# Moving the decode and attention steps that a decoder kernel weaves between its projection matmuls

## The reference

```python
x = _half_ffn(x, ffn1_norm, ffn1_in, ffn1_out)
h = _rmsnorm(x, mix_norm)
qa, ka, va, qr, kr, vr, gr, ga, gb = jnp.split(h @ w_in, SPLIT_POINTS, axis=-1)
...                       # QK norm, partial rotary
oa, kv_new = attend_a(qa, ka, va)      # dilated window attention, 3 groups x 8 heads x 64
orr, s_new = _retention(qr, kr, vr, s0, chunk)
ob = _rms_plain(orr).reshape(B, T, R_V_W) * jax.nn.silu(gr)
m = sigmoid(ga) * (oa.reshape(B, T, A_HEADS * A_HEAD_DIM) @ w_pa) + sigmoid(gb) * (ob @ w_pb)
x = x + (m @ w_o)
x = _half_ffn(x, ffn2_norm, ffn2_in, ffn2_out)
```

## Time and profile before

| | us |
|---|---|
| median of 3 runs (947.93 to 948.64) | 948.51 |
| the profiled execution | 948.64 |
| its span, first to last instruction | 946.8 |
| PE busy in it | 925.5 (98%) |
| PE's share of the chain that ended last | 78% |

### The profile page before, as it was taken

One profiled execution on the slowest core, in us unless ns is written; L12 is line 12 of the kernel. 1 busy time (PEld: TensorE's weight loads), 2 busy tenths in 40 slices (PEclk: granted clock), 3 DMA queues, 4 the chain that ended last, 5 costly groups with the idle time before them and its releaser, 6 DMA issues.

```text
span 946.8 us, 19298 instructions
## 1 busy us (share of the span) xinstructions
PE 925.5 (98%) x7863; PEld 875.9 (93%) x7863; DVE 610.5 (64%) x851; ACT 488.6 (52%) x752; POOL 222.6 (24%) x233
## 2 busy tenths in 40 slices
PE   9999999999999999899999999999999999999998
PEld 8999999999999888788788899779999999999998
DVE  6666655569955577677787744356756866666443
ACT  6444434454545655756665455337665744443332
POOL 0343330007700000267672104000001033333000
PEclk9999999999999999999999999999999999999999
DMA  9988879999988986889998787847787898887792
GB/s 359 385 311 311 295 259 338 321 378 367 322 278 289 331 310 226 297 333 411 320 340 291 258 288 249 275 146 267 267 289 269 310 312 281 318 296 248 261 377 96
DMA packets 62567, 281.15 MB, mean 297 GB/s; under 512 B 8176, under 2 KB 9328, under 8 KB 60880
## 3 DMA queue, kind: packets, MB, share of 16 engines
q1 hardware_dynamic: 23456, 148.31, 41.7%
q10 hardware_dynamic: 39024, 131.61, 41.4%
HBM read 256.64 MB, written 111.32 MB: 389 GB/s over the span
## 4 chain that ended last, share of the span: by engine, by line
PE 78%; DVE 9%; ACT 5%; DMA 4%; issue 3%; SPq 0%; ACTq 0%; POOL 0%; DVEq 0%
PE acc L408 14%; PE acc L410 14%; PE acc L409 14%; PE att L408 8%; PE att L409 8%; PE att L410 8%; DVE wl L388 2%; DMA raw<-w 1%; PE aux L798 1%; ACT wh L382 1%; PE att L842 1%; DVE state L974 1%; PE aux L983 1%; PE att L1034 1%; PE aux L1094 1%
## 5 line engine op out<-in xcount | busy, mean ns | idle before, releaser
L388 DVE TENSOR_TENSOR wl<-raw,wh 128x1024 fp32r<-128x1024 f32 (+2 forms) x280 | 336.1, 1202 | 238.7 <-ACT wh L382 233.5
L382 ACT ACTIVATE wh<-raw 128x1024 fp32r<-128x1024 f32 (+2 forms) x280 | 277.3, 993 | 210.7 <-PE acc L410 146.8
L408 PE MATMUL acc<-hh,wh 128*128 128x264 f32 x432 | 128.4, 297 | 0.1
L410 PE MATMUL acc<-hh,wl 128*128 128x264 f32 x432 | 122.5, 284 | 0.0
L409 PE MATMUL acc<-hl,wh 128*128 128x264 f32 x432 | 122.5, 284 | 0.0
L408 PE MATMUL acc<-xh,wh 128*128 128x264 f32 x416 | 118.8, 286 | 1.0 <-DVE wl L388 0.9
L408 PE MATMUL att<-xh,wh 128*128 128x264 f32 x416 | 118.5, 285 | 0.2 <-DVE wl L388 0.2
L409 PE MATMUL att<-xl,wh 128*128 128x264 f32 x416 | 117.9, 283 | 0.0
L409 PE MATMUL acc<-xl,wh 128*128 128x264 f32 x416 | 117.8, 283 | 0.0
L410 PE MATMUL att<-xh,wl 128*128 128x264 f32 x416 | 117.8, 283 | 0.0
L410 PE MATMUL acc<-xh,wl 128*128 128x264 f32 x416 | 117.8, 283 | 0.0
(11 more groups left out here) (255 smaller groups left out, 2001.8 us busy)
## 6 DMA issues: line engine op xcount, KB each, us to landing
raw<-w ACTq DMA_DIRECT2D x207, 512.0 KB, 6.5
state<-state_in SPq DMA_DIRECT2D x32, 512.0 KB, 7.8
state_out<-state SPq DMA_DIRECT2D x32, 512.0 KB, 6.2
raw<-w ACTq DMA_DIRECT2D x32, 384.0 KB, 6.6
kv<-cache SPq DMA_DIRECT2D x48, 256.0 KB, 4.5
raw<-w ACTq DMA_DIRECT2D x32, 320.0 KB, 5.7
raw<-w SPq DMA_DIRECT2D x9, 512.0 KB, 9.7
kv_out<-cache SPq DMA_DIRECT2D x3, 960.0 KB, 5.2
```

What stands on the lines that cost most here:

```text
L382: nc.scalar.activation(wh[n % HI_RING][:, 0:slot_size(n)], raw[n % RAW_RING][:, 0:slot_size(n)], ACT.Copy).then_inc(hi_done, 1)
L388: nc.vector.tensor_tensor(wl[n % RAW_RING][:, 0:slot_size(n)], raw[n % RAW_RING][:, 0:slot_size(n)], wh[n % HI_RING][:, 0:slot_size(n)].bi ...
L408: nc.tensor.matmul(out, w_hi, xh, start=first, stop=False)
L410: return nc.tensor.matmul(out, w_lo, xh, start=False, stop=last)
```

## The change

It moves steps, and changes no arithmetic and no count of instructions:

- PE, decode: `pe_dec_turn` goes from k0 of u2 to k5 of u1. The six value groups go from k7 of u2, twice k4 of u3, k5 of u4, twice k5 of u5 to k2 and k5 of u2, k3 of u3, k2 and k7 of u4, k5 of u5; the first now waits for all of `act_dec_turn`. `pe_dec_own` goes from k7 of u6 to k5 of u5, ahead of the last value group, and needs the first half's `v_own`; `pe_dec_gather` goes from k7 to k5 of u6. The sums of both move from bank 7 to bank 6.
- PE, attention: scores go from k2 to k1 of an item's first slot; the second half's transposes of the item before, which stood ahead of them, go to k4 of that slot. `pe_pv` goes from k3 to k0 of the second slot, and the first half's transposes, which stood behind it, to k7. `pe_pv` now writes a free part of bank 7 rather than the scores' bank 4, so its wait for the next item's mask, and the scores' wait for `act_pv`, go.
- DVE: the second half's `v_own` goes from u5 to u6, behind the `lo` of u5. `dve_dec_out` goes from u7 to u6. The mask of an item's first half comes ahead of `turned_copy` rather than behind it. The reciprocal of the first half goes from between the mask and the maximum of the second half into the second slot, behind the `lo` of the first slot.
- ACT: the first half's `act_prob` goes from the first slot into the second, behind the exponential of the second half and `act_pv`, and `turned_copy` behind both `act_prob`.

The core of the diff:

```diff
-        v_own = [at("v_own0", 93440, [AW]), at("v_own1", 91392, [AW])]
+        v_own = [at("v_own0", 16896, [AW]), at("v_own1", 91392, [AW])]
...
             if i:
                 pe.wait_ge(att_masked, 2 * i)
-                if i > 1:
-                    pe.wait_ge(att_out, i - 1)
...
         def pe_turn(pe, i, r):
             pe.wait_ge(att_prob, 2 * i + r + 1)
             if i == 0 and r == 0:
-                pe.wait_ge(v_own_done, 1)
-            elif r:
-                pe.wait_ge(att_turned_out, turned_copies(i, 0))
-            elif i == 1:
-                pe.wait_ge(dec_dve, DEC_DVE)
+                pe.wait_ge(dec_dve, DEC_DVE)
+            elif r == 0:
+                pe.wait_ge(att_out, i)
+            else:
+                pe.wait_ge(att_turned_out, turned_copies(i, 0))
...
         def pe_dec_own(pe):
-            pe.wait_ge(dec_act, 4)
-            pe.wait_ge(vs_out, AT)
-            pe.wait_ge(v_own_done, 2)
+            pe.wait_ge(v_own_done, 1)
...
         def pe_dec_v(pe, group):
             if group == 0:
-                pe.wait_ge(dec_act, 3)
+                pe.wait_ge(dec_act, 4)
...
         def dve_dec_own_rows(dve, half):
-            dve.wait_ge(dec_v_done, (4, 6)[half])
+            dve.wait_ge(dec_v_done, G * (half + 1))
...
         def pe_dec_gather(pe):
+            pe.wait_ge(v_own_done, 2)
...
-        DEC_V = {2: (7,), 3: (4, 4), 4: (5,), 5: (5, 5)}
+        DEC_V = {2: (2, 5), 3: (3,), 4: (2, 7), 5: (5,)}
```

More of the change, by code:

```diff
@@ L1123, in pe_pv @@
                     c = g * AW + (2 * pair + r) * AE
-                    last = nc.tensor.matmul(bank4[r * AE:(r + 1) * AE, 0:P], v_tok[:, kb, c:c + AE],
+                    last = nc.tensor.matmul(bank7[r * AE:(r + 1) * AE, 256:256 + P], v_tok[:, kb, c:c + AE],
                                             probT[:, r, n * P:(n + 1) * P], start=n == 0, stop=n == len(blks) - 1)
@@ L1130, in act_pv @@
             act.wait_ge(att_pv, i + 1)
-            nc.scalar.activation(oa[:, pair, qb * P:(qb + 1) * P], bank4[:, 0:P], ACT.Copy).then_inc(att_out, 1)
+            nc.scalar.activation(oa[:, pair, qb * P:(qb + 1) * P], bank7[:, 256:256 + P], ACT.Copy).then_inc(att_out, 1)
         def kv_rows(b, g, part):
@@ L1303, in pe_dec_gather @@
         def pe_dec_gather(pe):
+            pe.wait_ge(v_own_done, 2)
             for half in range(2):
                 for n in range(4):
-                    out = bank7[:, 256 + n * 16 + 8 * half:256 + n * 16 + 8 * half + 8]
+                    out = bank6[:, n * 16 + 8 * half:n * 16 + 8 * half + 8]
                     last = nc.tensor.matmul(out, v_own[half][:, n * P:(n + 1) * P], const("own_seq"),
@@ L1316, in dve_dec_out @@
                 nc.vector.tensor_copy(oa[rows, :, S:T].rearrange("p n (c b) -> p n c b", c=2),
-                                      bank7[rows, 256:320].rearrange("p (n c r b) -> p n c r b", n=4, c=2, r=2)[:, :, :, r]
+                                      bank6[rows, 0:64].rearrange("p (n c r b) -> p n c r b", n=4, c=2, r=2)[:, :, :, r]
                                       ).then_inc(dec_dve, 1)
@@ L1597, in att @@
                     if i < ATT:
+                        act_prob(act, i, 0)
+                        act_prob(act, i, 1)
                         turned_copy(act, i, 0, 0)
-                        act_prob(act, i, 1)
                 else:
@@ L1774, in att @@
                 else:
+                    if i < ATT:
+                        dve_scores(dve, i, 0)
                     if 1 <= i <= ATT:
@@ L1786, in _ @@
                     dve_dec_prob(dve)
-                if i == ATT_AT:
-                    dve_dec_own_rows(dve, 0)
-                    dve_dec_own_rows(dve, 1)
-                if i == ATT_AT + 2:
+                if i in (ATT_AT, ATT_AT + 1):
+                    dve_dec_own_rows(dve, i - ATT_AT)
+                if i == ATT_AT + 1:
                     dve_dec_out(dve)
@@ L1978, in att_steps @@
                     steps[1] += [lambda n=n: pe_key_score(pe, n) for n in range(B * G - 3, B * G)] + [lambda: pe_own_score(pe)]
-                if u == 2:
-                    steps[0].append(lambda: pe_dec_turn(pe))
+                if u == 1:
+                    steps[5].append(lambda: pe_dec_turn(pe))
+                if u == ATT_AT:
+                    steps[5].append(lambda: pe_dec_own(pe))
                 for n, k in enumerate(DEC_V.get(u, ())):
@@ L1983, in att_steps @@
                 if u == ATT_AT + 1:
-                    steps[7] += [lambda: pe_dec_own(pe), lambda: pe_dec_gather(pe)]
+                    steps[5].append(lambda: pe_dec_gather(pe))
                 if u < ATT_AT:
@@ L1988, in att_steps @@
                     if 1 <= i <= ATT:
-                        steps[3].append(lambda: pe_pv(pe, i - 1))
+                        steps[0].append(lambda: pe_pv(pe, i - 1))
                     if i < ATT:
-                        steps[3 if i else 7].append(lambda: pe_turn(pe, i, 0))
+                        steps[7].append(lambda: pe_turn(pe, i, 0))
                 else:
+                    if i < ATT:
+                        steps[1].append(lambda: pe_scores(pe, i))
                     if 1 <= i <= ATT:
-                        steps[2].append(lambda: pe_turn(pe, i - 1, 1))
-                    if i < ATT:
-                        steps[2].append(lambda: pe_scores(pe, i))
+                        steps[4].append(lambda: pe_turn(pe, i - 1, 1))
                 return steps
```

12 lines of the change are left out of this document (2 added, 10 removed).

## The result

The changed kernel takes **953.63 us** (median of 4 executions, 952.29 to 955.3), the kernel before beside it 948.22 (4 executions, 946.63 to 948.64): a ratio of 1.0061, interval 1.0041 to 1.0081. It is slower, by 5 us. The profiled execution took 954.19.

What follows compares the result with a forecast made beforehand. PE was taken to bound the kernel, busy for 925.5 of 946.8 us. 9.9 us comes and 5.0 goes, +4.9 on the profiled execution's 948.64, giving 953.5 us; range 950.6 to 955.7.

Steps and rivals of the forecast that it cites:

- low clock: Slow stretch after `pe_dec_own` and `pe_dec_gather`, side by side before: goes once full passes stand between them, 1.6 us off.
- (a): `pe_dec_turn`, nine passes earlier: PE stops early but starts at the same time, waiting for `dec_p`; +1.1 us.
- (b): First value group: PE waits for `act_dec_turn`, which on ACT stands behind the `hi` of u1; +1.25 us.
- (c): `pe_dec_own`: PE waits for the first half's `v_own`; +0.2 us (0 to 0.4).
- (d): `pe_dec_gather`: PE waits for the second half's `v_own`, now behind item 0's mask and the `lo`; +2.0 us (1.6 to 2.2).
- (e): Item 0's first transposes: wait for `dve_dec_out`, then reciprocal and `act_prob`; +0.45 us (0 to 0.6).
- (f): Odd items' transposes: wait because the reciprocal stands behind the second half, gate product and `lo`; +2.9 us (0.5 to 4).
- (g): 17 more places where PE changes between passes and steps: 0.9 decode, 1.1 attention, +2.0 us together (0.9 to 3.6).
- rival 4: A value group still waits for its transfer, a third of 3.0 us staying: +1.0, so 954.5 us; chance 0.08.
- rival 2: Low clock comes again around the gather, after PE idles 2.0 and gathers 1.95 us: 955.1 us; chance 0.25.
- Rival 1: New waits do not come, ACT and DVE reach each step in time: 945.6 us, faster; chance 0.02, its half 0.03.
- Rival 3: Odd items do not wait, PE's delay in the second slot being larger: 950.6 us; chance 0.10.

Runs made afterwards that it cites:

- `v_own` early: Changed kernel with the second half's `v_own` on DVE back ahead of item 0's mask, right behind the first half's: 953.89 us, ratio 1.0065.
- attention half alone: Kernel before with only the attention moves of the change, decode as before: 949.17 us, ratio 0.9998.
- `pe_dec_turn` back: Changed kernel with `pe_dec_turn` put back at k0 of u2: 952.59 us, ratio 1.0032.
- copies ahead: Changed kernel with ACT's `act_dec_turn` copies ahead of the `hi` of u1 rather than behind it: 954.54 us, ratio 1.0059.
- reciprocal early: Changed kernel with the first half's reciprocal behind the second half's scores, ahead of the gate product and the `lo`: 952.36 us, ratio 1.0049.
- decode half: Kernel before with only the decode moves of the change, attention as before: 956.19 us, ratio 1.0067.
- three edits: Changed kernel with `pe_dec_turn` back at k0 of u2, second half's `v_own` early and first half's reciprocal early: 949.53 us, ratio 0.9995.

## Why the prediction was right, point by point

It said 953.5 and slower. The time is 953.63. The mechanism held: moving PE's steps earlier moved none of their inputs, and PE stood. Term by term, from the two profiles. What a place costs is read from the start of the last pass ahead of it to the start of the second pass behind it, less two passes, and set against a like place without the wait or without the low clock:

| term | predicted | measured |
|---|---|---|
| transfer wait | -2.2 | -1.7 |
| waits for `act_prob` at the old places | -1.2 | -1.6 |
| low clock | -1.6 | +1.6, two stretches of 3.4 instead of one |
| (a) `pe_dec_turn` | +1.1 | +1.1 |
| (b) first value group | +1.25 | +1.45 |
| (c) `pe_dec_own` | +0.2 | +0.25 |
| (d) gather | +2.0 | +1.5 |
| (e) item 0's transposes | +0.45 | +0.7 |
| (f) odd items | +2.9 | +2.9 |
| (g) places, decode | +0.9 | +0.5 |
| (g) places, attention | +1.1 | -0.1 |
| sum | +4.9 | +6.6 (the section: +6.6) |

**(a), (b), (c)** were right in cause and size. The steps on DVE and ACT, each at its own place in its queue:

```profile
596.42 1.22 DVE L388 TENSOR_TENSOR wl<-raw,wh 128x1024 fp32r<-128x1024 f32 x1 [2.12 <-ACT wh L382]
...
597.76 0.42 DVE L1241 TENSOR_SCALAR dec_p<-dec_p,dec_m 128x387 f32<-128x387 f32 x1
...
628.66 1.22 DVE L388 TENSOR_TENSOR wl<-raw,wh 128x1024 fp32r<-128x1024 f32 x1 [0.32 <-ACT wh L382]
629.80 0.68 DVE L1287 TENSOR_TENSOR v_own<-aux,tab 128x512 f32<-128x512 f32 x1
...
643.81 0.22 DVE L1064 RECIPROCAL att_m<-att_m 128x1 f32<-128x1 f32 x2
```

`dec_p` ends at 598.18 and PE starts at 598.24; beside the whole profile's shift of 1.1 that is the same moment as before. `v_own` ends at 630.48, right behind the `lo`, and the gather starts at 630.54. The reciprocals follow the `lo` of u7, and ACT's `prob` of item 1 begins at 644.00.

**(d)** had the cause right and both sides too early. From the start t of the last value group I had let the chain end at t + 6.1 and PE arrive at t + 4.1. The group ran mostly at the low clock and took 1.74, the passes behind it 0.22 each: the chain ended at t + 6.9 (623.55 to 630.48), PE arrived at t + 5.6, and the wait was shorter by the difference.

**(f)** had 0.7, 0.7, 0.7 and 0.8 for items 1, 3, 5 and 7; measured were 0.4, 0.8, 0.8 and 0.9. The first transposes of item 3, with the passes on both sides:

```profile
664.00 0.29 PE L410 MATMUL acc<-obh,wl 128*128 128x264 f32 x1
664.88 0.88 PE L1089 MATMUL aux<-tab,prob 128*128 128x128 f32 x6 [0.59 <-ACT prob L1069]
665.51 0.37 PE L408 MATMUL acc<-obh,wh 128*128 128x264 f32 x1
665.72 0.29 PE L409 MATMUL acc<-obl,wh 128*128 128x264 f32 x1
```

From 664.00 to 665.72, less two passes, is 1.48; item 1's second transposes, six as well and without a wait, cost 0.66 (from 648.48 to 649.38, shown further down). So a wait that shows as 0.59 idle cost 0.82. For the same reason the old waits for `act_prob`, which I took at their idle time of 1.2, were worth 1.6. At item 1 PE came late from the second low stretch; with `v_own` early, where no low stretch lies behind the gather, item 1 lost 0.9 too. The cause, the reciprocal behind the `lo`, is shown by the edit that moved it.

**(g)** is mis-sized, in attention above all. I had read 0.19 per change of place from value groups. Scores that stand alone pay that too, 0.09 in and 0.11 out, and transposes 0.08 out. But steps of different kinds that share a place pay between each other as well, which two value groups side by side don't. Before, item 1's second transposes shared a place with the next scores:

```profile
642.19 0.28 PE L410 MATMUL acc<-obh,wl 128*128 128x264 f32 x1
642.37 0.88 PE L1094 MATMUL aux<-tab,prob 128*128 128x128 f32 x6
643.17 0.94 PE L1034 MATMUL att<-qk 64*128 64x128 f32 x12
644.04 0.39 PE L408 MATMUL acc<-obh,wh 128*128 128x264 f32 x1
644.27 0.28 PE L409 MATMUL acc<-obl,wh 128*128 128x264 f32 x1
```

That place cost 1.84. After, the scores alone cost 1.07 and the transposes 0.66, 1.73 together:

```profile
646.32 0.28 PE L410 MATMUL acc<-obh,wl 128*128 128x264 f32 x1
646.53 0.94 PE L1031 MATMUL att<-qk 64*128 64x128 f32 x12
647.40 0.39 PE L408 MATMUL acc<-obh,wh 128*128 128x264 f32 x1
647.63 0.29 PE L409 MATMUL acc<-obl,wh 128*128 128x264 f32 x1
...
648.48 0.28 PE L410 MATMUL acc<-obh,wl 128*128 128x264 f32 x1
648.60 0.82 PE L1089 MATMUL aux<-tab,prob 128*128 128x128 f32 x6
649.18 0.37 PE L408 MATMUL acc<-obh,wh 128*128 128x264 f32 x1
649.38 0.29 PE L409 MATMUL acc<-obl,wh 128*128 128x264 f32 x1
```

Value groups, in contrast, cost 2.05 for two at one place and 1.19 for one alone. The Trainium skill, TensorE: Matmul & The Clock Gate, section "Step-by-step: what each phase is for", has the next tile's weights load while this tile's matmul runs. By that no place would cost anything; here each change between passes and scores or value groups cost 0.09 on the way in and 0.10 on the way out, so the trace doesn't bear it out for these changes. Why a change of kind costs that isn't shown.

**The transfer** was rival 4 in part: with the groups spread, 0.4 to 1.1 us of wait stayed in eight of ten profiles, and none or 0.1 in two. As the wait varies as much at the old places, the -1.7 is the difference of two profiles and not shown to be the change's.

**The low clock** is the step that failed. I took 1.6 off since `pe_dec_own` and the gather were now apart, and gave rival 2, that it comes again, 0.25. Not one of the changed kernel's 11 executions had a clock of 1.000. In the profile it came twice, once behind each of the two, and each stretch cost 1.6 us against like steps at the full clock. That added 3.2 to the sum. I had also counted the slow stretch of before as a case of a wait that brings the low clock back; PE was busy all through the stretch ahead of it, 3.41 of 3.41. The places came out 1.6 lower than predicted, and the part ahead of the section was 1.1 shorter in this profile, which took most of it away. **So the number is right partly by luck**: the waits together were predicted at 4.5 and came to 4.6, the clock and the places were wrong by 3.2 and 1.6 in opposite directions. The clock's part is a comparison of two executions: before was profiled at a mean clock of 0.998, while 71 of the 87 others were at 0.996 or less, as the changed kernel's profile was. Rival 1 fell with (a). Rival 3 fell: all four items waited, the first of them for only 0.4.

## What to carry to other kernels

Before moving a step of the bound engine earlier, read who makes its input and what stands ahead of that in the producer's queue; if the consumer already waits there by a hair, as 0.19 us did here, every pass moved behind it becomes idle time. When the producer has a fixed piece of housekeeping in its queue (`hi` 1.06 us, `lo` 1.23), a 0.2 us reciprocal put behind it comes late by that piece: here it cost PE 0.8 us an item. And take several executions with their granted clock before explaining 2 us: here one low stretch more or less goes with about that.

## What was new about the chip

- **A few narrow matmuls cost more than their time.** `pe_dec_own` has weights of 8 x 128 and 16 columns moving; PE counts as busy, 3.21 of 3.40 us in the stretch that ends with it, and the granted clock then fell from 2.4 to 1.2 GHz. In all 13 profiles of kernels that have the step, the clock fell while it ran or within 2.5 us of its end. Left out, the clock stayed at 1.000 in six of six executions, and the kernel was 6.4 us shorter for 2.85 us of matmuls. Whether it is the 8 rows, the 16 columns or the length isn't shown.
- **Idle time may do the same.** In the attention half alone PE stood 2.07 us for a transfer, and the next stretch was at 0.53, with full passes in it; before, 1.81 us of standing, from 618.3 to 620.1, left the clock at 1.00 for the ten us behind it. Behind the gather it looks alike: in the six profiles in which PE waited ahead of it for 0.4 to 1.3 us (the changed kernel twice, `pe_dec_turn` back, copies ahead, reciprocal early, decode half) a low stretch began during the gather or within 2 us of its end, while with `v_own` early and with the three edits PE didn't wait there and none came. That is a coincidence in eight profiles, and no run tells the wait from the rest of the section. The two stretches of the attention half:

```profile
616.70:620.10 3.40, 1.33 (x14) 0.43 (x11) 0.13 (x1) 0.00 (x0) 0.00 (x0) 1.00 0.24 89
620.10:623.50 3.40, 3.40 (x18) 3.40 (x18) 3.26 (x8) 1.56 (x3) 0.00 (x0) 0.53 0.08 16
```

  The Trainium skill, TensorE: Matmul & The Clock Gate, section "HAM oscillation — how this bites in real kernels", tells of a kernel whose waits for transfers between bursts of matmuls brought the low clock back. The attention half's trace agrees, the kernel before's doesn't: a wait nearly as long had no such effect. And ahead of the narrow matmuls of before there is no wait, and the clock fell all the same.
- **The same program has several times.** Executions of one kernel on one chip spread over 945.3 to 954.7 us, with medians about 2 us apart from one mean clock to the next. Profiles also had a low stretch far from the section now and then (at 451.7 and 452.8 in one each, at 391.8 in a third); what causes those wasn't looked for.
- **A wait that goes doesn't always show in the time.** Each of the four single edits to the changed kernel took its wait away, all or most of it. One of them lowered the ratio to 1.0032 (`pe_dec_turn`), clear of the changed kernel's second measurement and not quite of its first; 1.0049 (reciprocal) overlaps with the changed kernel's, and the other two stayed at 1.0059 and 1.0065. For `v_own` early part of the wait came back at the next step of the same queue; for the rest the cause is open.
